# Two-block transformer in one kernel: the idle TensorE products between the stages are removed

## The chip, the cores and the metric

The kernel runs on one core of one Trainium2 chip. The metric is device microseconds of one execution, as a median over runs; smaller is better.

## The reference

Two blocks work on x of 256 tokens by 1024 channels, all in fp32. Cut to what matters here:

```python
def first_block(x, c, ...):
    for layer in range(2):
        shift, scale, gate = split(c @ mod_w[layer, 0] + mod_b[layer, 0], 3)
        h = rms_norm(x, norm_w[layer, 0, 0]) * (1.0 + scale) + shift
        y = mixer_ab(h, ...) if layer % 2 == 0 else mixer_cd(h, ...)
        x = x + gate * rms_norm(y, norm_w[layer, 0, 1])
        shift, scale, gate = split(c @ mod_w[layer, 1] + mod_b[layer, 1], 3)
        h = rms_norm(x, norm_w[layer, 1, 0]) * (1.0 + scale) + shift
        x = x + gate * rms_norm(swiglu(h, ffn_w_in[layer], ffn_w_out[layer]), norm_w[layer, 1, 1])

def second_block(x, cond, ...):          # mod: nine vectors from silu(cond) @ w_mod + b_mod
    x = x + 0.5 * g1 * swiglu_2(modulate(rms_norm_2(x, ffn1_norm), sh1, sc1), ...)
    proj = modulate(rms_norm_2(x, mix_norm), sh2, sc2) @ w_in
    y_mix = concat(rms_norm_2(short_conv(proj)), rms_norm_2(s5_mixer(proj)))
    x = x + g2 * (y_mix @ w_out)
    x = x + 0.5 * g3 * swiglu_2(modulate(rms_norm_2(x, ffn2_norm), sh3, sc3), ...)
    return rms_norm_2(x, final_norm)
```

What counts here is the shape: seven stages (ab, f0, cd, f1, f2, in2, f3), and between each and the next a normalisation over the 1024 channels of every token, on which the whole next stage depends.

## The kernel before

**Weights.** All weights and the matrices of the conditioning vectors come as one stream of 1 MB pieces through five buffers (`raw`), issued by SyncE in the order of a plan. ScalarE copies a half of a piece into `HI` in a rounded fp32 format, VectorE subtracts it from the original into `LO`; six such pairs are held. The conditioning vectors (`MV`) are made on VectorE by products of a raw piece with the condition and a sum (L1417). A product of weight and activation is three products on TensorE: both parts of the weight with the high part of the activation, and the high part of the weight with its low part.

**Activations.** `X` holds the rows of tokens. `HB` holds the modulated activation as high half (`HH`) and low half (`HLo`), in eight slices of 128 channels by 256 tokens; `HDH` and `HDL` hold the two parts of the hidden activation of a feed-forward stage.

**A stage change.** `add_normed` (or `add_gated`) adds the stage's result to `X` on VectorE. Then `modulate` runs on all engines. TensorE waits for the last gated bank (`gy`), transposes the 16 blocks of `X` into PSUM as each half of the rows is ready, and then spreads the inverse root of each half (`dg`, made by VectorE as a diagonal in `RS`) over all partitions with a product by a constant matrix (`nones`); these two are called the spreads here. ScalarE copies each spread back (`RS`), VectorE scales slice k by it (`TMP`, L1496), ScalarE writes `HH[k]`, VectorE writes `HLo[k]` (L1491), and TensorE begins the next stage as the slices appear. A feed-forward stage (f0 to f3) begins with one weight pair taken slice by slice, six products a slice; cd and in2 begin with one half, three products a slice.

**Idle products.** Before, `modulate` of TensorE also ran products whose result nobody reads, in four places: ahead of the wait for the first half, ahead of the second half's transposes, ahead of the second spread, and behind it. Their numbers are `fill`: (6, 4, 5, 4) at f0, cd, f1 and f2, (2, 2, 4, 4) at in2 and f3; the last is left out at f0. Each is 128 by 128 times 128 by 512, into a bank of the four that all stages share in turn (`take`, `give`). They wait for nothing themselves.

**Order.** Every engine's program is written out by hand in one order; TensorE takes its products strictly in that order.

Of the kernel before, what the change touches and what calls it, by code (L numbers as in the profile page):

```python
# [190 lines left out]
def build(nc, xT, small, vecs, ssm, consts, firsts, WS, scratch, gates_out, out):  # L191
# [15 lines left out]
    with ctx:  # L207
        def sb(name, shape, dt=fp32):
            return ctx.enter_context(nc.sbuf_tensor(name, shape, dt))

        def tally(name):
            return Tally(nc, ctx, name)
# [11 lines left out]
        HH, HLo = HB[:, 0], HB[:, 1]  # L224
        nones = sb("nones", [128, 128])
        zeros = sb("zeros", [128, 128])
        zb = zeros[:, :].bitcast(mybir.dt.bfloat16)
# [7 lines left out]
        HDH = sb("HDH", [128, 3, 256], f32r)  # L235
# [7 lines left out]
        P, A, D, G = tally("pe_done"), tally("act_done"), tally("dve_done"), tally("pool_done")  # L243
# [7 lines left out]
        banks = Banks(NWORK)  # L251
# [7 lines left out]
        def C(n):  # L259
            o, w = co[n]  # L260
            return CN[:, o:o + w]
# [13 lines left out]
        def turned(k):  # L275

            return PS[:, k % 4, k // 4 * 256:k // 4 * 256 + 256]
# [20 lines left out]
        def flat(a):  # L298
            return a.rearrange("p a b -> p (a b)")
# [106 lines left out]
        def pe(e):  # L406
            w = Waits(e)
            walk = Walk(plan, units, where, order)
            idle = [0]
            opened = set()  # L410

            def mm(o, l, r, start, stop):
                return e.matmul(o, l, r, start=start, stop=stop, skip_group_check=True)  # L413

            def freed(key):
                return D.at(("free", key)) if ("free", key) in D.value else A.at(("free", key))

            def take(key):
                i = banks.take(key)
                last = banks.before[key]  # L420
                if last is not None and last[0] != "idle":
                    w.wait_ge(*freed(last))
                return PS[:, WORK0 + i, :]

            def busy_wide(n, src=HH):
                idle[0] += 1
                key = ("idle", idle[0])
                ps = take(key)
                for i in range(n):
                    mm(ps[:, :], src[:, 0, 0:128], flat(src[:, 0:2, :]), True, True)  # L430
                banks.give(key)

            def busy(n):
                idle[0] += 1
                key = ("idle", idle[0])
                ps = take(key)
                w.wait_ge(*G.at("zeros"))
                for i in range(2 * n):
                    mm(ps[:, 0:256], zb[:, 0:128], zb, True, True)
                banks.give(key)  # L440

            def mods(col):
                walk.mods(col)

# [87 lines left out]
                if last:  # L532
                    x.then_inc(*P.up(("sum", tag)))

            def modulate(tag, sc, fill=(0, 0, 0, 0)):

                mods(sc + 8)
                if tag != "ab":
                    busy_wide(fill[0])
                    w.wait_ge(*D.at(("gy", tag, 3)))  # L540
                for qt in range(2):
                    if tag == "ab":
                        w.wait_ge(*XIN.at("in"))
                        w.wait_ge(*CONST.at("in"))
                    elif qt:
                        busy_wide(fill[1])
                    for k in range(8):
                        if tag != "ab" and k % 4 == 0:
                            w.wait_ge(*D.at(("x", tag, qt, k // 4)))
                        e.transpose(turned(k)[:, qt * 128:qt * 128 + 128], X[:, qt, k * 128:k * 128 + 128], C("ident"))  # L550
                for qt in range(2):
                    if qt and tag != "ab":
                        busy_wide(fill[2])
                    ps = take(("rb", tag, qt))
                    w.wait_ge(*D.at(("dg", tag, qt)))
                    mm(ps[:, 0:128], nones[:, :], dg[:, qt, :], True, True).then_inc(*P.up(("rb", tag, qt)))
                    banks.give(("rb", tag, qt))
                if tag not in ("ab", "f0"):
                    busy_wide(fill[3], HDH)

            def ffn(tag, slow, gcol):
                def down(j):
# [99 lines left out]
            def out_half(name, ks, qt, gives=1, begins=0):  # L662

                def half_ready(k):
                    wt = weight((name, k // 2), k % 2)
                    w.wait_ge(*A.at(("hh", name, k)))
                    w.wait_ge(*D.at(("hlo", name, 7 if qt or begins else max(k, 3))))
                    if begins and not qt:
                        w.wait_ge(*D.at(("hlo", name, 3)))
                    return wt  # L670

                ends = ks[-1] == 7 and qt == gives
                for k in ks[:-2] if ends else ks:
                    wt = half_ready(k)
                    rows(name, (HH, HLo), k, wt, k == begins, k == 7, [used((name, k // 2), k % 2)] if qt == gives else [],
                         (qt,))
                if ends:
                    wts = [half_ready(k) for k in ks[-2:]]
                    for h in range(2):
                        for k, wt in zip(ks[-2:], wts):  # L680
                            rows(name, (HH, HLo), k, wt, k == begins, k == 7,
                                 [used((name, k // 2), k % 2)] if h else [], (qt,), (h,))
# [4 lines left out]
            for q, oh in enumerate(("ohA", "ohB")):  # L687
                ps = take(("tab", q))
# [3 lines left out]
            walk.catch_up(walk.at_unit[4, 1])  # L692
            w.wait_ge(*G.at("consts"))
            modulate("ab", 8)

            for n in range(6):
# [3 lines left out]
            ps = take("gates")  # L700
            w.wait_ge(*D.at("gatew"))
            for k in range(8):
                mm(ps[0:24, 0:256], wgh[:, k, :], HH[:, k, :], k == 0, False)
                mm(ps[0:24, 0:256], wgl[:, k, :], HH[:, k, :], False, False)
                i = mm(ps[0:24, 0:256], wgh[:, k, :], HLo[:, k, :], False, k == 7)
            i.then_inc(*P.up("gates"))
            banks.give("gates")
            ps = take("gates2")
            w.wait_ge(*A.at(("free", "gates")))
            w.wait_ge(*CONST.at("in"))  # L710
            for qt in range(2):
                i = e.transpose(ps[:, qt * 24:qt * 24 + 24], ge[:, qt * 128:qt * 128 + 128], C("ident")[0:24, 0:24])
# [88 lines left out]
            out_half("abo", (0, 1), 1)  # L801
            out_half("abo", (6, 7), 0)
            out_half("abo", range(2, 8), 1)
            modulate("f0", 32, (6, 4, 5, 4))
            ffn("f0", lambda j: None, 40)

            opened.clear()
            modulate("cd", 56, (6, 4, 5, 4))
            for i in range(6):
                linear_fm(("cd", i), H2, "cd", 8, 2)  # L810

# [61 lines left out]
            out_half("cdo", (4, 5), 0, 0, 4)  # L873
            out_half("cdo", (0, 1, 2, 3, 6, 7), 0, 1, 4)
            out_half("cdo", (0, 1, 2, 3, 6, 7), 1, 1, 4)
            modulate("f1", 80, (6, 4, 5, 4))

            def turn(j):
                if j in (5, 6, 9, 10, 13, 14, 17, 18):
# [19 lines left out]
                    banks.give("kk")  # L899

            ffn("f1", turn, 88)
            modulate("f2", 104, (6, 4, 5, 4))
            ffn("f2", lags, 112)
            modulate("in2", 128, (2, 2, 4, 4))

            def drive():

# [50 lines left out]
            ps = take(("xs", "conv"))  # L958
# [8 lines left out]
            ps = take(("xs", "ssmy"))  # L967
# [2 lines left out]
            banks.give(("xs", "ssmy"))  # L970
            out_half("o2", range(4, 8), 0)
            out_half("o2", range(4, 8), 1)
            modulate("f3", 152, (2, 2, 4, 4))
            ffn("f3", lambda j: None, 160)

        def act(e):
# [1200 lines left out]
        for engine in (pe, act, dve, pool, sp):  # L2177
            engine(Counting())
# [5 lines left out]
        @block.tensor  # L2184
        def _(e):
            pe(e)
# [162 lines left out]
```

## Time and profile before

| | |
|---|---|
| median of 3 runs | 1234.2 us (1233.76 to 1235.08) |
| profiled execution | span 1233.6 us; the page gives no time of its own beside it |
| TensorE busy | 1145.4 us, 93% |
| VectorE busy | 957.4 us, 78% |
| ScalarE busy | 602.1 us, 49% |
| mean granted clock of TensorE | 0.976 |

The busy share of TensorE is by modelled ends of pipelined products; the start-to-start distance of rows tells more. The granted clock is given as a share of full speed: 1.00 is 2.4 GHz, 0.50 is 1.2 GHz, and a share between them is a stretch in which it changed. In the timeline a row may merge several instructions (x6); its second number is from the first start to the last end.

### The profile page before, as it was taken

What the parts mean: (1) busy time and instruction counts of PE and PEld (TensorE: products, weight loads), DVE (VectorE), ACT (ScalarE), POOL (GpSimd) and SP (SyncE); (2) the same over time, 40 slices, a digit from 0 to 9 for tenths busy, and PEclk for the clock granted to TensorE, in tenths of its full rate; (3) what the DMA queues carried; (4) which work ended last, traced back from release to release, by engine and by line L of the source; (5) the groups of instructions that cost most, each with busy time, mean ns of one, the idle gap of its engine ahead of it and who ended that gap; (6) DMA issues with size and microseconds to landing.
All of it is one profiled execution on the core that took longest, in us unless ns stands there. A gap on an engine that the chain in (4) does not pass through costs nothing.

```text
span 1233.6 us, 19573 instructions
## 1 busy us (share of the span) xinstructions
PE 1145.4 (93%) x8036; PEld 1023.9 (83%) x8036; DVE 957.4 (78%) x1710; ACT 602.1 (49%) x1055; POOL 69.4 (6%) x106
## 2 busy tenths in 40 slices
PE   2697899899999998999999999999999989999996
PEld 1696578899897996898998989999979968888885
DVE  5888868898887966788888778887776867777655
ACT  2434755444356457644344564344453365555543
POOL 1000000000000000185000000000000000000000
PEclk8799899999999999999999999999999999999998
DMA  9993334778882960367889637888723552666731
GB/s 374 358 391 126 133 127 181 305 304 312 290 336 108 368 263 21 131 261 273 306 245 360 249 108 277 327 283 313 302 94 126 111 181 86 217 260 253 183 128 35
DMA packets 41097, 280.74 MB, mean 228 GB/s; under 512 B 4768, under 2 KB 5296, under 8 KB 8240
## 3 DMA queue, kind: packets, MB, share of 16 engines
q1 hardware_dynamic: 37584, 269.27, 59.7%
q0 software_dynamic: 2416, 7.92, 2.0%
q10 hardware_dynamic: 1008, 2.30, 0.6%
q8 instruction: 63, 1.03, 0.3%
q14 instruction: 26, 0.21, 0.1%
HBM read 277.85 MB, written 1.10 MB: 226 GB/s over the span
## 4 chain that ended last, share of the span: by engine, by line
PE 64%; DVE 23%; ACT 6%; DMA 5%; issue 2%; SPq 0%; DVEq 0%; ACTq 0%
PE PS L413 64%; DVE LO L1427 7%; DMA raw<-WS 5%; DVE raw L1417 5%; ACT HI L981 3%; DVE TMP L1496 1%; DVE HB L1491 1%; DVE SC L1659 1%; ACT SQ L981 1%; DVE FB L1615 1%; DVE TMP L1533 1%; DVE TMP L1775 1%; DVE X L1538 1%; DVE SC L1644 1%; ACT HB L981 1%
## 5 line engine op out<-in xcount | busy, mean ns | idle before, releaser
L413 PE MATMUL PS<-HB,HI 128*128 128x256 f32 (+1 forms) x3160 | 648.2, 298 | 28.7 <-ACT HB L981 18.6
L413 PEld LDWEIGHTS PS<-HB,HI 128*128 128x128 f32 x3160 | 509.6, 192 | 57.0 <-ACT HB L981 21.1
L413 PE MATMUL PS<-HB,LO 128*128 128x256 f32 x1748 | 494.2, 283 | 0.0
L1427 DVE TENSOR_TENSOR LO<-raw,HI 128x1024 fp32r<-128x1024 f32 x340 | 404.1, 1226 | 92.7 <-ACT HI L981 92.6
L981 ACT ACTIVATE HI<-raw 128x1024 fp32r<-128x1024 f32 x340 | 338.5, 1047 | 91.6 <-DMA raw<-WS 44.9
L413 PEld LDWEIGHTS PS<-HB,LO 128*128 128x128 f32 x1748 | 334.8, 192 | 2.7
L1417 DVE CUSTOM_DVE_ANT_0 raw<-raw,CB,SM 128x1024 f32<-128x1024 f32 x168 | 209.9, 1284 | 18.9 <-DMA raw<-WS 18.8
L981 ACT ACTIVATE HDH<-FB 128x256 fp32r<-128x256 f32 x88 | 36.8, 418 | 243.9 <-DVE FB L1615 220.3
L413 PE MATMUL PS<-HI,HDH 128*128 128x512 f32 x352 | 140.2, 398 | 0.0
L413 PE MATMUL PS<-HI,HDL 128*128 128x512 f32 x352 | 139.4, 396 | 0.0
L413 PE MATMUL PS<-LO,HDH 128*128 128x512 f32 x352 | 139.1, 395 | 0.0
L413 PE MATMUL PS<-HI,HB 128*128 128x512 f32 (+2 forms) x352 | 91.6, 349 | 7.0 <-DVE HB L1516 5.9
L413 PEld LDWEIGHTS PS<-HI,HDL 128*128 128x128 f32 x352 | 66.4, 189 | 16.0
L1618 DVE TENSOR_TENSOR HDL<-FB,HDH 128x256 fp32r<-128x256 f32 x88 | 37.9, 430 | 51.6 <-ACT HDH L981 51.6
L413 PEld LDWEIGHTS PS<-HI,HDH 128*128 128x128 f32 x352 | 66.4, 189 | 13.5
L413 PEld LDWEIGHTS PS<-LO,HDH 128*128 128x128 f32 x352 | 66.4, 189 | 12.9
L413 PEld LDWEIGHTS PS<-HI,HB 128*128 128x128 f32 x352 | 62.2, 194 | 17.5 <-ACT HB L981 6.4
L981 ACT ACTIVATE FB<-PS 128x256 f32<-128x256 f32 (+1 forms) x115 | 45.2, 393 | 46.5 <-PE PS L413 46.2
L981 ACT ACTIVATE SC<-PS 128x512 f32<-128x512 f32 (+3 forms) x57 | 31.4, 567 | 63.5 <-PE PS L413 52.1
L413 PE MATMUL PS<-LO,HB 128*128 128x512 f32 (+2 forms) x176 | 61.0, 347 | 0.0
L2068 POOL DMA_DIRECT2D gates_out<-GV x7 | 6.4, 921 | 602.6 <-DVE GV L1511 343.4
L413 PE MATMUL PS<-SC 128*64 128x256 f32 (+4 forms) x336 | 36.3, 363 | 2.6 <-DVE SC L1659 1.5
(233 smaller groups left out, 925.0 us busy)
## 6 DMA issues: line engine op xcount, KB each, us to landing
raw<-WS SPq DMA_DIRECT2D x255, 1024.0 KB, 5.4
SC<-scratch POOLq DMA_DIRECT2D x2, 1024.0 KB, 16.0
FB<-gates_out POOLq DMA_DIRECT2D x3, 512.0 KB, 5.0
SQ<-gates_out POOLq DMA_DIRECT2D x3, 512.0 KB, 9.2
X<-xT ACTq DMA_DIRECT2D x1, 1024.0 KB, 6.8
SC<-ssm POOLq DMA_DIRECT2D x2, 512.0 KB, 3.8
out<-TMP SPq DMA_DIRECT2D x4, 256.0 KB, 2.6
CB<-vecs SPq DMA_DIRECT2D x1, 512.0 KB, 6.5
```

What stands on the lines that cost most here:

```text
L413: return e.matmul(o, l, r, start=start, stop=stop, skip_group_check=True)
L981: return e.activation(o, a, f, **k)
L1417: e.tensor_tensor_reduce(x, x, CB[:, :], 1.0, S("mb")[:, c:c + 1], O.mult, O.add, MV[:, c:c + 1]) \
L1427: e.tensor_tensor(LO[:, s % HL, :], raw_half(j, h), HI[:, s % HL, :].bitcast(fp32), O.subtract).then_inc(*D.up(("lo", s)))
L1491: e.scalar_tensor_tensor(HLo[:, k, :], TMP[:, k, :], MV[:, sh + k:sh + k + 1], HH[:, k, :].bitcast(fp32), O.add, O.subtract).then_inc(*D.u ...
L1496: e.scalar_tensor_tensor(TMP[:, k, :], turned(k), AV[:, k:k + 1], RS[:, 3, :], O.mult, O.mult) \
L1533: e.tensor_tensor(gy[b // 2][:, c], PS[:, b, :], grow(tag)[:, c], O.mult).then_inc(*D.up(("gy", tag, b)))
L1538: e.scalar_tensor_tensor(X[:, qt, c], gy[qt][:, c], r_n[:, qt:qt + 1], X[:, qt, c], O.mult, O.add) \
L1615: e.tensor_tensor(HF[:, j % 2, :], SIL[:, j % 2, :], bank((key, 0))[:, 256:512], O.mult) \
L1618: e.tensor_tensor(HDL[:, j % 3, :], HF[:, j % 2, :], HDH[:, j % 3, :].bitcast(fp32), O.subtract) \
L1644: e.tensor_scalar(s3[:, n, :], s3[:, n, :], gg[:, n:n + 1], None, O.mult) \
L1659: e.tensor_tensor_reduce(s3[:, n, :], bank(("s", tag, i))[:, n * kw:(n + 1) * kw], reverse(BI[:, bh + h0 + n, 0:kw]), 1.0, sk[:, n:n + 1] ...
```

## The change

`modulate` on TensorE no longer takes `fill`, and runs no idle product. Both helpers, `busy_wide` and the unused `busy`, are deleted. Nothing else is edited.

```diff
-            def busy_wide(n, src=HH):
-                idle[0] += 1
-                key = ("idle", idle[0])
-                ps = take(key)
-                for i in range(n):
-                    mm(ps[:, :], src[:, 0, 0:128], flat(src[:, 0:2, :]), True, True)
-                banks.give(key)
...
-            def modulate(tag, sc, fill=(0, 0, 0, 0)):
+            def modulate(tag, sc):
 
                 mods(sc + 8)
                 if tag != "ab":
-                    busy_wide(fill[0])
                     w.wait_ge(*D.at(("gy", tag, 3)))
                 for qt in range(2):
                     if tag == "ab":
                         w.wait_ge(*XIN.at("in"))
                         w.wait_ge(*CONST.at("in"))
-                    elif qt:
-                        busy_wide(fill[1])
                     for k in range(8):
...
                 for qt in range(2):
-                    if qt and tag != "ab":
-                        busy_wide(fill[2])
                     ps = take(("rb", tag, qt))
...
-                if tag not in ("ab", "f0"):
-                    busy_wide(fill[3], HDH)
...
-            modulate("f0", 32, (6, 4, 5, 4))
+            modulate("f0", 32)
...
-            modulate("in2", 128, (2, 2, 4, 4))
+            modulate("in2", 128)
```

The order of TensorE at the change to f2, before: the last products of f1 (those that read HDH with HI or LO), then idle products (reading HB or HDH alone) among the transposes (CN,X) and the spreads (RS,nones), then the first products of f2.

```order
L413 MATMUL PS<-HI,HDL 128x512
L413 MATMUL PS<-HB 128x512 x6
L550 MATMUL PS<-CN,X 128x128 x8
L413 MATMUL PS<-HB 128x512 x4
L550 MATMUL PS<-CN,X 128x128 x8
L413 MATMUL PS<-RS,nones 128x128
L413 MATMUL PS<-HB 128x512 x5
L413 MATMUL PS<-RS,nones 128x128
L413 MATMUL PS<-HDH 128x512 x4
L413 MATMUL PS<-HB,HI 128x256
```

The same place of the change:

```order
L413 MATMUL PS<-HI,HDL 128x512
L530 MATMUL PS<-CN,X 128x128 x16
L413 MATMUL PS<-RS,nones 128x128 x2
L413 MATMUL PS<-HB,HI 128x256
L413 MATMUL PS<-HB,LO 128x256
```

Nineteen products are gone there, and nothing has moved in their place. The change to f3, before, on TensorE, between the last product of the mixer's output and the first of f3:

```order
L413 MATMUL PS<-HI,HB 128x512
L413 MATMUL PS<-HB 128x512 x2
L550 MATMUL PS<-CN,X 128x128 x8
L413 MATMUL PS<-HB 128x512 x2
L550 MATMUL PS<-CN,X 128x128 x8
L413 MATMUL PS<-RS,nones 128x128
L413 MATMUL PS<-HB 128x512 x4
L413 MATMUL PS<-RS,nones 128x128
L413 MATMUL PS<-HDH 128x512 x4
```

And of the change:

```order
L413 MATMUL PS<-HI,HB 128x512
L530 MATMUL PS<-CN,X 128x128 x16
L413 MATMUL PS<-RS,nones 128x128 x2
L413 MATMUL PS<-HB,HI 128x256
L413 MATMUL PS<-HB,LO 128x256
```

Twelve products are gone there. The other engines' instructions and waits are the same, in the same order.

## Rows read from the trace of the kernel before

**Rows 1.** The page: its head, and the chain's shares by engine.

```profile
span 1233.6 us, 19573 instructions
...
PE 64%; DVE 23%; ACT 6%; DMA 5%; issue 2%; SPq 0%; DVEq 0%; ACTq 0%
```

**Rows 2.** The chain in order of time: start us, us, what (longest pieces).

```profile
200.00 1.20 DVE raw L1417
...
317.31 13.53 DMA raw<-WS
...
522.80 3.58 DVE LO L1427 x3
...
718.25 190.70 PE PS L413 x1383
...
1049.33 174.07 PE PS L413 x904
```

**Rows 3.** Instructions by tile, HB and HDH, TensorE: duration ns min/median/max.

```profile
L413 PE MATMUL PS<-HB x76: 387/393/481, 183.6 to 1034.6; 128*128 128x512 f32 x76
...
L413 PE MATMUL PS<-HDH x20: 387/397/478, 393.1 to 1035.8; 128*128 128x512 f32 x20
```

**Rows 4.** Stretches: length, busy PE, PEld, DVE, ACT, POOL, clock, DMA, GB/s.

```profile
44.80:48.10 3.30, 2.12 (x11) 1.34 (x11) 3.12 (x7) 3.02 (x6) 0.00 (x0) 1.00 0.84 348
48.20:51.50 3.30, 3.30 (x17) 3.30 (x17) 3.30 (x5) 1.85 (x2) 0.00 (x0) 0.50 0.72 253
...
709.90:718.20 8.30, 7.32 (x40) 5.32 (x38) 5.66 (x21) 4.80 (x18) 0.00 (x0) 1.00 0.00 0
```

**Rows 5.** Timeline at the change to f2: second spread, its reader, first product.

```profile
716.16 0.49 PE L413 MATMUL PS<-RS,nones 128*128 128x128 f32 x2
...
716.69 0.28 ACT L981 ACTIVATE RS<-PS 128x128 f32<-128x128 f32 x1 [1.23 <-PE PS L413]
...
718.25 0.36 PE L413 MATMUL PS<-HB,HI 128*128 128x256 f32 x1 [0.68 <-ACT HB L981]
```

**Rows 6.** Timeline at the start, low clock: second spread and its reader.

```profile
26.21 0.80 PE L413 MATMUL PS<-RS,nones 128*128 128x128 f32 x2 [1.13 <-DVE RS L1477]
27.04 0.28 ACT L981 ACTIVATE RS<-PS 128x128 f32<-128x128 f32 x1 [1.55 <-PE PS L413]
```

**Rows 7.** Timeline of TensorE in stage ab at the low clock.

```profile
41.78 0.41 PE L413 MATMUL PS<-HB,LO 128*128 128x256 f32 x1
...
42.57 0.42 PE L413 MATMUL PS<-HB,LO 128*128 128x256 f32 x1
...
48.43 0.63 PE L413 MATMUL PS<-HB,HI 128*128 128x256 f32 x2
...
49.07 0.63 PE L413 MATMUL PS<-HB,HI 128*128 128x256 f32 x2
```

**Rows 8.** Timeline of TensorE in f2: first pair by slices, then unheld.

```profile
720.29 0.47 PE L413 MATMUL PS<-HB,HI 128*128 128x256 f32 x2
...
721.07 0.47 PE L413 MATMUL PS<-HB,HI 128*128 128x256 f32 x2
...
724.58 0.40 PE L413 MATMUL PS<-HB,HI 128*128 128x256 f32 x2
...
724.94 0.40 PE L413 MATMUL PS<-HB,HI 128*128 128x256 f32 x2
```

**Rows 9.** Timeline at the change to in2: second spread's input and its product.

```profile
912.52 0.28 DVE L1477 TENSOR_SCALAR RS<-CN,NR 128x128 f32<-128x128 f32 x1
...
913.16 0.38 PE L413 MATMUL PS<-RS,nones 128*128 128x128 f32 x2
```

**Rows 10.** Timeline: f0's first reader, and waits of TensorE in f1, f3.

```profile
201.97 0.36 ACT L981 ACTIVATE FB<-PS 128x256 f32<-128x256 f32 x1
...
572.19 0.36 PE L413 MATMUL PS<-HB,HI 128*128 128x256 f32 x1 [1.66 <-DVE LO L1427]
...
1049.33 0.50 PE L413 MATMUL PS<-HB,HI 128*128 128x512 f32 x1 [0.24 <-DVE FB L1615]
```

More of the change, by code:

```diff
@@ L423, in take @@
                 return PS[:, WORK0 + i, :]
-            def busy_wide(n, src=HH):
-                idle[0] += 1
-                key = ("idle", idle[0])
-                ps = take(key)
-                for i in range(n):
-                    mm(ps[:, :], src[:, 0, 0:128], flat(src[:, 0:2, :]), True, True)
-                banks.give(key)
[L433 to L440, printed above, removed]
             def mods(col):
@@ L803, in pe @@
             out_half("abo", range(2, 8), 1)
-            modulate("f0", 32, (6, 4, 5, 4))
+            modulate("f0", 32)
             ffn("f0", lambda j: None, 40)
             opened.clear()
-            modulate("cd", 56, (6, 4, 5, 4))
+            modulate("cd", 56)
             for i in range(6):
@@ L875, in pe @@
             out_half("cdo", (0, 1, 2, 3, 6, 7), 1, 1, 4)
-            modulate("f1", 80, (6, 4, 5, 4))
+            modulate("f1", 80)
             def turn(j):
@@ L901, in pe @@
             ffn("f1", turn, 88)
-            modulate("f2", 104, (6, 4, 5, 4))
+            modulate("f2", 104)
             ffn("f2", lags, 112)
-            modulate("in2", 128, (2, 2, 4, 4))
+            modulate("in2", 128)
             def drive():
@@ L972, in pe @@
             out_half("o2", range(4, 8), 1)
-            modulate("f3", 152, (2, 2, 4, 4))
+            modulate("f3", 152)
             ffn("f3", lambda j: None, 160)
```

## The prediction

> **What bounds the kernel now.** I read the page first, for the bound; then the chain in order of time, for which engine carries it in each stage; then, at the six stage changes, the timeline of each engine and the granted clock by stretches. The page puts 64% of the chain on TensorE and 23% on VectorE [rows 1]. The chain in order tells the stages apart [rows 2]. In stage f2 TensorE carries it for 190.70 us without a break, and in f3 for the last 174.07 us: a microsecond lost there is lost for good. In f0 and f1 it runs over VectorE right behind the stage change (VectorE's conditioning products at 200.00, low halves of weights at 522.80), and in f0 later over a weight transfer of 13.53 us. There TensorE has time to spare.
>
> At a stage change TensorE has nothing of use to do for 8.30 us (f2, 709.90 to 718.20) but 16 transposes and two spreads, and the idle products fill the rest; the clock stays at 1.00 throughout [rows 4]. There are 96 idle products, 76 that read HB and 20 that read HDH [rows 3].
>
> **The change, part by part.** No engine but TensorE has another instruction or another wait. What is left of the gap is 16 transposes and two spreads of two passes each.
>
> *Does the clock fall?* The nearest rows are at the program's start [rows 4]. From 44.80 to 48.10 TensorE ran 11 products of 256 columns, busy for 2.12 us by the profile and idle for 1.18 us in all, and from 48.20 to 51.50 its clock was 0.50. Eleven products of 0.11 us of streaming (256 columns at 2.4 GHz) are 1.2 us of work in 3.3 us. At f2 the gap will hold 16 transposes and 4 passes of 128 columns, 20 x 0.053 = 1.1 us of work in 8.30 us: less than half of that density. So I take it that the clock falls at all six changes; at in2 and f3, whose gaps are some 2 us shorter, it falls late. The Trainium skill ("TensorE: Matmul & The Clock Gate", section "Why this matters for your kernels") warns only of idle gaps longer than any that this change leaves; by it alone the clock would stay up. The start rows speak against that, since 1.18 us without work, among thin work, was enough there.
>
> *Term A, the spread.* The second spread stands on the chain at every change: ScalarE waits for it, VectorE for ScalarE. At the full clock it takes 716.16 to 716.69, 0.53 us [rows 5]; at the low clock, at the start, 26.21 to 27.04, 0.83 us [rows 6]. That is 0.30 us more. At f2 it comes 6.3 us into the gap (709.90 to 716.16), and much the same at f0, cd and f1; I take the clock to be low by then. In cd and f2 it is lost in full. In f0 and f1 the chain meets later stalls that may swallow it (the 13.53 us transfer); I take half. Together 0.30 x 2 + 0.15 x 2 = 0.90 us. Bounds: 0 (clock still up) and 1.8 (six times).
>
> *Term B, the first weight pair of f2.* Six products belong to each of the eight slices of the modulated activation, and VectorE releases the slices: the same product stands at 720.29 and 721.07, 0.78 us a slice. Unheld, three products take 0.36 us (724.58 to 724.94), so 0.72 us a slice [rows 8]. At the low clock three products take 0.64 us (48.43 to 49.07) [rows 7], so 1.28 us a slice. With the clock low for D us after the first product, the pair ends at D + (8 - D/1.28) x 0.72 = 5.76 + 0.44 D; released by VectorE it ends at 7 x 0.78 + 0.72 = 6.18. The loss is 0.44 D - 0.42. The low stretch from 48.20 took 3.3 us, and the one before it reached from ahead of 41.78 to 44.80 at most; I bound D by 4.0. At f2 part of the low stretch will be over when work begins, so I take 3.0: 0.90 us. Bounds: 0 (D up to 1) and 1.34 (D of 4.0).
>
> *Term C, the same pair of f3.* Same sum, 0.90 us, less a stall that it fills: behind the third weight pair TensorE now idles 0.24 us until VectorE frees a bank [rows 10]. So 0.66 us. Bounds 0 and 1.1.
>
> *The same pairs of f0 and f1* cost nothing. In f0 the first reader of the result, ScalarE's at 201.97, stands behind other work of ScalarE and does not wait for TensorE; in f1 TensorE itself idles 1.66 us for a low half of weights at 572.19 [rows 10]. If that cover were gone, each would cost as much as f2's, 0.9 us.
>
> *cd and in2* begin with three products a slice, 0.64 us at the low clock, under the 0.78 us of the release. The start shows it: at the low clock the same product stands at 41.78 and 42.57, 0.79 us apart [rows 7]. Cost 0.
>
> *Term D, what the idle products hold up.* In in2 VectorE has the second spread's input at 912.52 + 0.28 = 912.80, but TensorE begins it at 913.16, behind idle products [rows 9]; without them it would follow at once, for which I allow 0.05 us. So 0.31 us is won, and the same at f3, where the timeline reads alike: -0.62 us together. At f2 nothing is held. Bounds: -0.62, and 0 if the clock is already low there.
>
> **Sum.** 0.90 + 0.90 + 0.66 - 0.62 = +1.84 us. On the profiled execution, of which the page gives only the span, that is 1233.6 to 1235.4 us; the median of the runs, 0.6 above the span, goes from 1234.2 to 1236.0 us, 0.15% more. Ends: all bounds low -0.6 (1233.6), all high 1.8 + 1.34 + 1.1 = +4.2 (1238.4).
>
> The Trainium skill weighs it otherwise: the same page, section "Terms", prices low clock at the throttled time times one minus the ratio, so half of it. With 3.3 us for each of six stretches that is six times 1.65, about 9.9 us, against the 1.84 of the rows. The start rows disagree for cd and in2: 0.79 us a slice at the low clock where f2 has 0.78 at the full one.
>
> **The rivals.**
>
> *All of it passes (slower).* The low stretch of every change delays the end by half its length, as if nothing were released or waited for elsewhere: 6 x 3.3 / 2 = 9.9 us, 1244.1 us. For it: in f2 and f3 the chain is all TensorE. Against: VectorE carries the chain in f0 and f1, and releases the slices in cd and in2. It decides where a slice at the low clock outlasts the release by much and no wait follows.
>
> *Cover is thinner than it looks (slower).* The pairs of f0 and f1 pass on to the end (2 x 0.9), and the spread's 0.30 passes in full (2 x 0.15): 1.84 + 2.1 = +3.9, 1238.1 us. For it: in f1 TensorE is nearly full as well, ahead of that wait. Against: up to 572 the timelines of f1 name no wait of ScalarE or VectorE on TensorE. It decides from a delay beyond 1.66 us in f1.
>
> *The clock stays up (no change by measure).* Transposes and spreads are enough to keep it. Then only term D is left: 1233.6 us. For it: the gap is broken up by that work, with no long pause left in it. Against: the fall at 48.2.
>
> *Idle products disturb others (faster).* If they slow VectorE's or ScalarE's steps in the gap, these get shorter. VectorE is busy for 5.66 us of f2's gap [rows 4]; a tenth of that, six times, is 3.4 us: 1230.8 us. No row shows such a slowing.
>
> **How the numbers follow.** Repeated runs lie within about 0.1% (1233.76 to 1235.08), and about 0.2%, 2.5 us, is what a measurement of this kernel can tell from no change. The sum as worked out: 0.50. Clock stays up: 0.13. Thinner cover: 0.23. All passes: 0.10. Faster: 0.04. Within 0.2% falls the forecast but for a tail of 0.04, and the clock that stays up, 0.59 in all; slower 0.23 + 0.10 + 0.04 = 0.37; faster 0.04. The range goes from 1233.4 (clock up) to 1238.8 (thinner cover), and leaves out the first and the last rival and some edge. The likeliest case alone: 1234.8 to 1237.2. Predicted: 1236.0 us.
>
> **What would show it.** In the profile of the changed kernel: no product that reads HB or HDH alone; a clock of 0.50 in stretches that begin inside the six gaps and end a few microseconds after the first weight product; 0.83 us from the second spread to ScalarE at f0, cd, f1, f2 (A); first pairs of f2 and f3 of about 7 us instead of 6.2 (B, C); in cd and in2 slices of 0.79 us at either clock; in in2 and f3 the second spread 0.05 us behind VectorE (D); in f0 and f1 the waits for low halves shorter by as much as the first pair got longer. Wrong it would be by a clock of 1.00 in the gaps, by low stretches of 6 us and more after work begins, by a second fall while slices are still being released, or by a wait in f0 or f1 of ScalarE or VectorE on TensorE that is not there now.

## The result and the profile after

| | before | changed |
|---|---|---|
| first comparison, median of 5 runs each | 1234.2 us (1233.55 to 1235.08) | 1239.33 us (1237.98 to 1240.87) |
| ratio, with its 95% interval | | 1.0032 [1.0019, 1.0046] |
| the same kernel again, 12 runs | 1235.71 us (35 runs) | 1238.54 us, ratio 1.0020 [1.0005, 1.0035] |
| a third time, 11 runs | 1236.08 us (23 runs) | 1237.6 us, ratio 1.0012 [1.0003, 1.0021] |

The forecast was 1236.0 us, with a range up to 1238.8. The first comparison lies above it. The three ratios, weighted by the inverse square of their intervals, give 1.0019 [1.0012, 1.0025]: some 2.3 us of 1234.2, against the 1.84 of the sum. The second and the third were taken on different chips, and the intervals of the first and the third overlap by little, so the pooled one is rough. Both halves of that need explaining: why the first comparison showed 5.1 us between the medians, and whether 2.3 us came about as the prediction had it.

The profiled execution of the changed kernel took 1239.33 us, of which 1237.5 lie in the span, so 1.8 us lie around it. Before, I had only a span of 1233.6 [rows 1] and a median 0.6 above it; if 1.8 us lie around that span too, that execution took 1235.4 us, and the two profiles differ by 3.9 us only. The page of the changed kernel, its head and the chain's shares:

```profile
span 1237.5 us, 19376 instructions
...
PE 61%; DVE 25%; DMA 6%; ACT 6%; issue 2%; SPq 0%; DVEq 0%; ACTq 0%
```

TensorE's share of the chain is 61% where it was 64%. The chain in order of time, for the pieces that answer to [rows 2]: start, length, what.

```profile
318.46 14.07 DMA raw<-WS
...
720.08 192.69 PE PS L413 x1383
...
1053.30 174.07 PE PS L413 x904
```

The same 1383 products of f2 take 192.69 us instead of 190.70: 1.99 us, half of the whole difference, in one row. The 904 products of f3 take 174.07 in both, and they start 3.97 us later. The weight transfer at 318 took 14.07 us instead of 13.53; nothing in the change touches it.

The stretches at the change to f2, which answer to [rows 4]: length, busy time of PE, PEld, DVE, ACT and POOL, granted clock, DMA.

```profile
711.90:720.00 8.10, 3.43 (x21) 2.29 (x20) 5.51 (x20) 4.60 (x18) 0.00 (x0) 0.94 0.00 0
719.10:722.40 3.30, 2.32 (x10) 2.30 (x11) 3.11 (x8) 1.93 (x4) 0.00 (x0) 0.50 0.00 0
722.50:725.80 3.30, 3.30 (x17) 3.30 (x17) 3.12 (x9) 2.42 (x5) 0.00 (x0) 0.50 0.00 0
725.90:729.20 3.30, 3.30 (x29) 3.30 (x29) 1.69 (x3) 3.27 (x4) 0.00 (x0) 1.00 0.18 22
```

TensorE is busy for 3.43 us of the gap, where the idle products had made it 7.32. The clock falls at the very end of the gap, about 719.0, and is still 0.50 in the second low row, although TensorE had work all through it (3.30 of 3.30). It is back at 725.9. The first product of f2 starts at 720.08, so the clock is low for 5.8 us of work. The timeline there, of TensorE and of ScalarE's reader, beside [rows 5] and [rows 8]:

```profile
718.08 0.49 PE L413 MATMUL PS<-RS,nones 128*128 128x128 f32 x2 [1.02 <-DVE RS L1453]
718.61 0.28 ACT L957 ACTIVATE RS<-PS 128x128 f32<-128x128 f32 x1 [1.23 <-PE PS L413]
720.08 0.58 PE L413 MATMUL PS<-HB,HI 128*128 128x256 f32 x1 [1.51 <-ACT HB L957]
...
721.41 0.63 PE L413 MATMUL PS<-HB,HI 128*128 128x256 f32 x2
...
722.69 0.63 PE L413 MATMUL PS<-HB,HI 128*128 128x256 f32 x2
...
726.24 0.40 PE L413 MATMUL PS<-HB,HI 128*128 128x256 f32 x2
...
726.60 0.40 PE L413 MATMUL PS<-HB,HI 128*128 128x256 f32 x2
```

The spread still ran at the full clock here (0.53 us to ScalarE, as before). Then a slice takes 1.28 us (721.41 to 722.69), which is the price that the prediction read from the start of the program, and three products are back at 0.36 us from 726.24. At cd the spread came late enough to meet the low clock (VectorE's input, the spread, the reader):

```profile
394.18 0.29 DVE L1453 TENSOR_SCALAR RS<-CN,NR 128x128 f32<-128x128 f32 x1
394.52 0.80 PE L413 MATMUL PS<-RS,nones 128*128 128x128 f32 x2 [0.68 <-DVE RS L1453]
395.35 0.28 ACT L957 ACTIVATE RS<-PS 128x128 f32<-128x128 f32 x1 [1.20 <-PE PS L413]
```

That is 0.83 us, to the hundredth what [rows 6] gave. At in2 the spread now follows its input by 0.05 us (916.33 + 0.29 = 916.62, then 916.67), where [rows 9] had 0.36. The last row below is the stall of f3 that answers to [rows 10]: 0.23 us where it was 0.24.

```profile
916.33 0.29 DVE L1453 TENSOR_SCALAR RS<-CN,NR 128x128 f32<-128x128 f32 x1
916.67 0.49 PE L413 MATMUL PS<-RS,nones 128*128 128x128 f32 x2 [0.94 <-DVE RS L1453]
...
1053.30 0.49 PE L413 MATMUL PS<-HB,HI 128*128 128x512 f32 x1 [0.23 <-DVE FB L1591]
```

The stretches at cd, f1, in2, and the gap and first pair of f3:

```profile
391.40:401.50 10.10, 7.86 (x30) 6.89 (x31) 7.89 (x23) 5.85 (x15) 0.00 (x0) 0.50 0.00 0
510.90:521.00 10.10, 7.92 (x33) 7.31 (x34) 7.89 (x24) 5.84 (x15) 0.53 (x1) 0.50 0.15 52
920.50:923.70 3.20, 3.14 (x13) 2.73 (x12) 3.20 (x9) 2.09 (x5) 0.00 (x0) 0.50 0.00 0
1034.20:1040.70 6.50, 2.99 (x22) 2.30 (x20) 4.46 (x16) 3.51 (x12) 0.53 (x1) 1.00 0.21 81
1040.80:1046.80 6.00, 5.98 (x45) 5.71 (x46) 5.59 (x14) 4.07 (x8) 0.00 (x0) 1.00 0.02 4
```

At cd and f1 the clock is low for 10.1 us in a row, three times the 3.3 that the prediction went by. At f3 it does not fall at all, in a gap with 2.99 us of busy TensorE in 6.50.

### The profile page after: what moved, and what is told of

Same layout as the page of the kernel before. It is cut to its first block, busy times and chain, and to the rows that moved or that the text cites. A ratio compares the mean times of both kernels' runs of the same rounds, so it can differ in the third digit from the quotient of the medians.

```text
span 1237.5 us, 19376 instructions
## 1 busy us (share of the span) xinstructions
PE 1137.1 (92%) x7940; PEld 1020.1 (82%) x7940; DVE 956.7 (77%) x1710; ACT 603.7 (49%) x1055; POOL 69.5 (6%) x106
## 4 chain that ended last, share of the span: by engine, by line
PE 61%; DVE 25%; DMA 6%; ACT 6%; issue 2%; SPq 0%; DVEq 0%; ACTq 0%
PE PS L413 60%; DVE LO L1403 8%; DVE raw L1393 6%; DMA raw<-WS 6%; ACT HI L957 3%; DVE TMP L1472 1%; DVE SC L1635 1%; DVE HB L1467 1%; PE PS L612 1%; ACT SQ L957 1%; DVE FB L1591 1%; DVE TMP L1509 1%; DVE X L1514 1%; ACT HB L957 1%; ACT HDH L957 1%
## 5 line engine op out<-in xcount | busy, mean ns | idle before, releaser
L413 PEld LDWEIGHTS PS<-HB,HI 128*128 128x128 f32 x3160 | 515.4, 194 | 55.0 <-ACT HB L957 24.9
L413 PEld LDWEIGHTS PS<-HB,LO 128*128 128x128 f32 x1748 | 338.9, 194 | 2.7
L413 PE MATMUL PS<-SC 128*64 128x256 f32 (+4 forms) x336 | 38.8, 380 | 3.1 <-DVE SC L1635 1.5
## 6 DMA issues: line engine op xcount, KB each, us to landing
SQ<-gates_out POOLq DMA_DIRECT2D x3, 512.0 KB, 10.2
```

## The experiments

Each was compared with the kernel before on the same chip (e1 to e4 on one, a2 and e5 to e7 on a second, a3, e8 and b2 on a third); the diffs are against the kernel before. One table serves them all. It splits every profiled execution into stages, at the start of the last weight product of each stage, so that a gap belongs to the stage behind it (f3 ends with the last product of the program; o2 is in2 and the mixer's output). A star marks a stage whose idle products were left out or cut.

```
kernel    ab ends     f0      cd      f1      f2      o2      f3
before     183.41  202.90  118.75  204.57  198.92  121.41  193.03
e1         182.76  203.01  118.45  204.37  198.90  121.36  193.04
b2         184.39  203.06  118.35  204.59  198.93  121.20  192.85
e2         183.68  203.01  118.39  204.58  200.85* 121.47  193.04
e3         182.06  203.32* 118.20  205.05* 198.89  122.34  193.03
e4         184.72  204.13  118.34* 204.47  198.89  121.17* 193.42*
e5         182.21  203.03  118.53  204.90  199.69* 122.22  193.05
e6         183.81  203.06* 119.00* 205.43* 198.91  120.76* 193.38*
e7         183.36  203.54  118.42  204.51  198.92  119.36* 193.58*
e8         182.31  203.00  118.71  204.60  200.83* 121.93  193.04
changed    184.63  203.37* 118.93* 204.63* 200.80* 121.76* 192.84*
a2         185.82  203.29* 118.83* 205.16* 200.66* 121.27* 192.85*
a3         184.04  203.34* 118.26* 204.89* 200.63* 121.34* 192.76*
```

f2 is the clearest column: 198.89 to 198.93 us in the seven profiles with all its idle products, 200.63 to 200.85 in the five that lack those around the second spread (with or without the earlier ones), and 199.69 in e5, which lacks the earlier ones alone. Stage ab, ahead of every edit, ends anywhere from 182.06 to 185.82. The columns f0, cd, f1 and o2 scatter too where nothing of them was edited: f0 from 202.90 to 204.13, cd from 118.20 to 118.75, f1 from 204.37 to 204.90, o2 from 121.20 to 122.34.

**e1, the kernel before once more.** A copy, no edit.

> The kernel before once more, for a second profile. Theory: 1.2 us of the change's 5.1 us are no effect of the change but where the clock falls in stage ab, which no idle product precedes; then this profile has low stretches in stage ab at other places than the first profile of it, and f0's first product comes at a time that differs from the first profile's by 0.5 to 1.5 us. Rival: stage ab falls alike in every execution of this kernel and the changed kernel shifts it; then f0's first product stands within 0.2 us of the first profile's.

The first product of f0 came at 191.79 us, against 192.45 in the first profile of the kernel before. Stage ab ended 0.65 us earlier, and its long low stretches stood elsewhere (101.6 to 111.9 us and 118.7 to 125.5, against 123.3 to 130.1). So where the clock falls in stage ab differs between executions of one kernel; that much of the theory holds. The execution took 1234.3 us, with a span of 1232.5.

**e2, left out at f2 alone.**

```diff
-            modulate("f2", 104, (6, 4, 5, 4))
+            modulate("f2", 104)
```

> The idle products left out at the change to f2 alone. Theory (terms A and B with the low stretch lasting 5.8 us behind the first product, as the trace of the change has it): 0.30 + 0.44 x 5.8 - 0.42 = +2.4 us, 1.0020 of the kernel before, with a clock of 0.50 for 6 to 7 us from about 1 us after f2's first weight product or around it. As predicted (low for 3.0 us behind it): +1.2 us, 1.0010. Rival, all of a low stretch passes: half of 6.8 us, +3.4 us, 1.0028. Rival, the clock stays up: 0.

Ratio 1.0013 [1.0004, 1.0022], 1.6 us. The clock was low from the gap until 723.7 us, 5.1 us past the first product of f2 (718.58). The stretch of that work, and the chain's piece that it opens:

```profile
718.60:723.60 5.00, 5.00 (x23) 5.00 (x24) 5.00 (x13) 3.06 (x7) 0.00 (x0) 0.50 0.02 3
```

```profile
718.58 192.35 PE PS L413 x1383
```

The ratio alone does not choose between the theory's 1.0020 and the prediction's 1.0010; the rows do: 192.35 - 190.70 = 1.65 us for the pair and 0.30 us more gap make the 1.95 of the table. The formula of term B gives 0.44 x 5.1 - 0.42 = 1.82. The clock that stays up is excluded; that all of the low stretch passes (3.4 us) lies outside the interval.

**e3, left out at f0 and f1 alone.**

```diff
-            modulate("f0", 32, (6, 4, 5, 4))
+            modulate("f0", 32)
...
-            modulate("f1", 80, (6, 4, 5, 4))
+            modulate("f1", 80)
```

> The idle products left out at the changes to f0 and f1 alone. Theory: the first weight pairs are covered, by ScalarE's other work in f0 and by the wait for a low half of weights in f1, and only half of the second spread's 0.30 us is left at each: +0.3 us, 1.0002, with the wait in f1 at the low half of weights shorter by the lag of the first pair. Rival, the cover is thinner: 2 x (0.30 + 0.90) = +2.4 us with the low stretch as predicted, up to 2 x 2.4 = +4.8 us with that of f2, 1.002 to 1.004.

Ratio 1.0002 [0.9994, 1.0011]. Here both second spreads met the low clock (both gaps were 0.30 us longer), and both first pairs ran at it, for 4 to 5 us. The wait in f1 shows where the rest went:

```profile
571.00 0.36 PE L413 MATMUL PS<-HB,HI 128*128 128x256 f32 x1 [0.75 <-DVE LO L1427]
```

It had been 1.66 us [rows 10], and is 0.75 here (0.57 in the changed kernel): TensorE came late, and waited less. From the first product of f1 to its last the stage took 195.62 us, against 195.24 to 195.46 in the three profiles of the kernel before. The cover held but for 0.2 to 0.4 us. The rival's +2.4 us and more lies outside the interval (up to +1.4).

**e4, left out at cd, in2 and f3 alone.**

```diff
-            modulate("cd", 56, (6, 4, 5, 4))
+            modulate("cd", 56)
...
-            modulate("in2", 128, (2, 2, 4, 4))
+            modulate("in2", 128)
...
-            modulate("f3", 152, (2, 2, 4, 4))
+            modulate("f3", 152)
```

> The idle products left out at the changes to cd, in2 and f3 alone. Theory: 0.30 us for the second spread at cd, nothing for cd's and in2's first halves, -0.31 us each at in2 and f3 for the second spread that is no longer held up, and at f3 0 or 0.66 us as the clock falls there or not: -0.3 to +0.3 us, 0.9997 to 1.0003. Rival, all of the low stretches passes: cd 5.1 us, in2 1.7 us, f3 1.7 us, in all +5 to +8.5 us, 1.004 to 1.007. Rival, stage o2 and f3 pass on what in2 and cd lose: +1.5 us, 1.0012.

Ratio 0.9999 [0.9990, 1.0008]: the theory's 0.9997 to 1.0003, and neither rival. The gaps of in2 and f3 were 0.19 us shorter each (term D). And at f3 the clock did fall this time, but only behind the first product (1038.40):

```profile
1031.90:1038.30 6.40, 2.89 (x21) 2.29 (x20) 4.36 (x16) 3.51 (x12) 0.53 (x1) 1.00 0.24 82
1038.50:1039.60 1.10, 1.10 (x8) 0.94 (x8) 1.10 (x4) 0.55 (x2) 0.00 (x0) 1.00 0.03 7
1039.80:1043.00 3.20, 3.20 (x17) 3.20 (x17) 3.20 (x9) 2.04 (x4) 0.00 (x0) 0.50 0.00 0
```

In the middle row TensorE is at work without a pause at clock 1.00, and then it drops for the 3.2 us of the last row. From the first product of f3 to the last took 186.74 us, against 186.16: 0.58 us. That is term C, where the clock falls.

**a2, the changed kernel once more.** A copy, no edit.

> The changed kernel once more, with more rounds. Theory: of the first comparison's 5.1 us only the part that the stages behind a removed group show is the change's (f2 1.9, f0, cd, f1 and in2 0.2 to 0.4 each, f3 -0.2 to +0.4), the rest is where the clock falls in stage ab, which differs from one execution to the next of the kernel before too (its end at 182.1 to 184.7 us in five profiles): +2 to +3 us, 1.0016 to 1.0025. Rival, the whole 5.1 us is the change's: 1.0035 to 1.0045 again, and stage ab ends at 184.5 us or later again.

Ratio 1.0020 [1.0005, 1.0035], as the theory had it; but stage ab ended late again (185.82 us), as the rival had it, so the cause stayed open and a3 below repeats it. Its f2, and that of a3, as pieces of the chain:

```profile
721.93 192.25 PE PS L413 x1383
```

```profile
719.36 192.22 PE PS L413 x1383
```

1.55 and 1.52 us more than before, with a clock low for 4.8 us (until 726.7) and 4.7 us (until 724.1) behind the first product.

**e5, at f2 only the late idle products.**

```diff
-            modulate("f2", 104, (6, 4, 5, 4))
+            modulate("f2", 104, (0, 0, 5, 4))
```

> At the change to f2 the idle products ahead of the transposes left out (6 and 4), those around the second spread kept (5 and 4). Theory, only the clock behind f2's first weight product counts (term B): the 9 late products either keep it up, then 0, 1.0000, or they come too late to bring it back, then the 1.9 us of all being left out, 1.0016, with a clock of 0.50 over some 5 us behind the first product. Rival, what costs is the thin work of the whole gap: about half of it, +1 us, 1.0008.

Ratio 1.0006 [0.9991, 1.0021], too wide to choose; the trace chooses. f2 took 199.69 us, 0.79 more than before, and none of it behind the first product: the 1383 products took 190.71 us. The clock fell inside the gap and was back before them:

```profile
712.30:715.60 3.30, 3.30 (x14) 2.94 (x14) 2.10 (x9) 1.98 (x7) 0.00 (x0) 0.50 0.00 0
715.80:718.00 2.20, 1.60 (x8) 0.98 (x7) 0.93 (x3) 0.87 (x3) 0.00 (x0) 1.00 0.00 0
718.10:724.00 5.90, 5.90 (x44) 5.64 (x45) 5.55 (x14) 3.96 (x8) 0.00 (x0) 1.00 0.01 3
```

The rival's size, about 1 us, was near; what cost the 0.8 us neither had: the five idle products ahead of the second spread ran at the low clock, took 2.10 us and held the spread up. Its input was there at 714.86 + 0.29 = 715.15; it began at 716.08.

```profile
714.86 0.29 DVE L1477 TENSOR_SCALAR RS<-CN,NR 128x128 f32<-128x128 f32 x1
```

```profile
714.14 2.10 PE L413 MATMUL PS<-HB 128*128 128x512 f32 x5
716.08 0.38 PE L413 MATMUL PS<-RS,nones 128*128 128x128 f32 x2
```

**e6, left out everywhere but at f2** (the edits of e3 and e4 together).

> The change with the idle products of f2 kept, all others left out. Theory: f2 is the only change where they are worth anything; what is left is the second spread at f0, f1 and cd and the gain of term D: 0 to +0.9 us, 1.0000 to 1.0007. Rival, the parts pass on more together than alone (stage f0 and f1 lose their cover when cd and in2 come late): +2 us or more, 1.0016.

Ratio 1.0005 [0.9990, 1.0019], median 1235.81 against 1235.71: what the theory had, 0 to 0.9 us, but with +2 us (1.0016) inside the interval. The stages that carry a star sum, against the mean of the three profiles of the kernel before, to 203.06 + 119.00 + 205.43 + 120.76 + 193.38 - (202.99 + 118.52 + 204.51 + 121.32 + 192.97) = +1.3 us, of which f1 is 0.9.

**e7, more idle products where the clock falls in the kernel before, fewer where they hold up.**

```diff
-            modulate("in2", 128, (2, 2, 4, 4))
+            modulate("in2", 128, (2, 2, 2, 4))
...
+            busy_wide(6, HDH)
             linear_out("o2", range(4))
...
+            busy_wide(14, HDH)
             out_half("o2", range(4, 8), 0)
...
-            modulate("f3", 152, (2, 2, 4, 4))
+            modulate("f3", 152, (2, 2, 2, 4))
```

> The kernel before with more idle products, where its own trace has the clock fall: 6 ahead of the first and 14 ahead of the last four channel slices of the mixer's output (TensorE waits 1.94 us at 1000.13 and 3.91 us at 1017.63 there, and the clock is 0.50 for 3.4 us from each), and 2 in place of 4 ahead of the second spread of in2 and f3. Theory: both low stretches are on the chain of TensorE and cost half their length, 2 x 1.7 us, and term D gives 2 x 0.3 us: -4.0 us, 0.9968. Rival, what TensorE gains there it waits for again: only term D, -0.6 us, 0.9995. Rival, the added products hold up the slices: 0 or slower.

Ratio 0.9995 [0.9980, 1.0009]: the theory's 4 us did not come; median 1234.63 against 1235.71. The two low stretches are gone (in the kernel before the clock was 0.50 from 1000.5 and from 1017.6, 3.4 us each):

```profile
998.00:1001.00 3.00, 2.44 (x12) 1.74 (x11) 2.09 (x5) 0.81 (x2) 0.00 (x0) 1.00 0.01 3
1013.00:1017.30 4.30, 3.65 (x16) 2.66 (x15) 2.29 (x6) 1.31 (x3) 0.00 (x0) 1.00 0.78 318
1017.40:1021.00 3.60, 3.60 (x16) 2.97 (x17) 2.15 (x6) 1.60 (x4) 0.00 (x0) 1.00 0.00 0
```

Stage o2 became 2.0 us shorter and f3 0.6 us longer, because its gap grew to 7.42 us from 6.87: TensorE was done sooner, and its transposes waited 1.35 us for VectorE where they had waited 0.63. From the last product of f2 to the first of f3 it took 126.78 us, against 128.07 to 128.28 in the three profiles of the kernel before: 1.3 to 1.5 us less, of which 0.2 are in2's shorter gap and 0.29 the second spread of f3. So neither the theory's 4.0 us nor the rival's 0.6: TensorE waits again for the greater part of what the clock gives it.

**a3, the changed kernel a third time.** A copy, no edit.

> The changed kernel a third time, beside runs on another chip perhaps. Theory (the sum of what the changed stages showed: f2 1.9, cd 0.3, f1 0.5, o2 -0.5, f3 0.1, f0 0): +2.2 us, 1.0018, and stage ab, in which nothing differs, ends between 182 and 186 us as it falls out (182.1 to 184.7 us in the eight profiles of kernels that keep idle products at f2 or elsewhere, 184.6 and 185.8 in the two of the changed kernel). Rival, stage ab is really later in the changed kernel: its end at 184.5 us or later a third time, and +4 us, 1.0032.

Ratio 1.0012 [1.0003, 1.0021], with the theory's 1.0018 inside and the rival's 1.0032 outside. Stage ab ended at 184.04 us. The three changed profiles end it at 184.04 to 185.82, the three of the kernel before at 182.76 to 184.39, and the other seven, with the same program up to there, at 182.06 to 184.72.

**e8, at f2 only the early idle products.**

```diff
-            modulate("f2", 104, (6, 4, 5, 4))
+            modulate("f2", 104, (6, 4, 0, 0))
```

> At the change to f2 the 10 idle products ahead of the transposes kept, the 9 around the second spread left out. Theory (what counts is how long the clock is 0.50 behind the first weight product): the work just ahead of f2's first product is as thin as without any, so the clock falls at or behind that product and stays low for some 3.4 us or more behind it: stage f2 at 199.5 to 200.7 us against 198.9 with all of them, +0.6 to +1.8 us, 1.0005 to 1.0015. Rival, the early products are enough: 198.9 us, 1.0000.

Ratio 1.0012 [1.0004, 1.0021], and f2 at 200.83 us: the ten early products bought nothing at all.

```profile
709.00:716.10 7.10, 5.28 (x31) 3.82 (x29) 4.64 (x19) 4.09 (x16) 0.00 (x0) 1.00 0.00 0
716.30:717.20 0.90, 0.00 (x0) 0.00 (x0) 0.71 (x3) 0.61 (x2) 0.00 (x0) 0.50 0.00 0
717.30:722.90 5.60, 5.60 (x26) 5.60 (x27) 5.41 (x14) 3.66 (x8) 0.00 (x0) 0.50 0.01 3
```

```profile
717.24 0.55 PE L413 MATMUL PS<-HB,HI 128*128 128x256 f32 x1 [1.60 <-ACT HB L981]
...
717.24 192.62 PE PS L413 x1383
```

TensorE was busy for 5.28 of the first 7.10 us. Behind the second spread it stood still for 1.60 us, the clock fell in that pause, and then it was low for 5.8 us of full work (until 723.0). Loss 1.92 us, a little more than the 0.6 to 1.8 expected; the formula gives 2.13. The nine products behind the early ones are what f2 needs, and by e5 they need the early ones ahead of them.

**b2, the kernel before a third time.** A copy, no edit.

> The kernel before a third time, for a profile. Theory: stage ab ends anywhere between 182 and 186 us; f2 takes 198.9 us and f3 193.0 us as in the other profiles with all idle products there, and stage f1 204.4 to 204.6 us.

Stage ab ended at 184.39 us, f2 took 198.93, f1 204.59, and f3 192.85, 0.2 under what was expected. The execution took 1235.79 us, 1.5 us more than e1's of the same kernel, and stage ab's 1.63 us account for it. This kernel has all its idle products, and yet its clock fell behind the first products of f0 (193.43) and of in2 (915.91):

```profile
195.40:198.60 3.20, 3.20 (x17) 3.20 (x17) 3.20 (x9) 2.08 (x5) 0.00 (x0) 0.50 0.00 0
919.10:922.30 3.20, 3.20 (x13) 2.85 (x13) 2.55 (x7) 2.64 (x5) 0.00 (x0) 0.50 0.00 0
```

So did that of e2 at f0 (from 194.6) and that of e3 at in2 (from 916.5), which keep the products there.

## Why the prediction was right or wrong

**The size.** The range was exceeded by the first comparison, and not by the two later ones taken by their ratios (1234.2 x 1.0020 and x 1.0012 are 1236.7 and 1235.7 us). Of the 5.1 us between the first medians, the trace showed 1.2 us lost before f0 began, where the program is the same, and 0.5 us in one weight transfer. By the means of three profiles each, the stages behind that differ by f0 +0.3, cd +0.2, f1 +0.4, f2 +1.8, o2 +0.1 and f3 -0.2: together 2.6 us, which fits the pooled 2.3. That the rest was where the clock happened to fall in stage ab is not shown: the changed kernel's three ends of ab are 1.3 us later in the mean than those of the kernel before, 1.6 us later than the mean of all ten profiles in the rows above them in the table, of which only e4's is later than 184.63. Spreads of 1.6 to 1.8 us don't settle whether that is chance. The whole times speak for chance: 2.6 us behind ab and 1.3 in it would be 3.9, and the pooled interval ends at 3.1.

**Does the clock fall?** "At all six changes" held at f0, cd, f1, f2 and in2, in all three profiles, in the gap or up to 2 us behind it. It failed at f3: the clock stayed up there in all three, and fell at f3 in e4 and e6, which lack the same products there. So the same gap can go both ways. Nor do the idle products decide it alone: at cd, f1 and f2 no profile that keeps all of them shows a fall, but at f0 two of eight do (e2, b2), and at in2 two of seven (e3, b2). Those falls came 1.9 to 3.1 us behind the first product, and those at in2 in the changed kernel's profiles 1.1 to 1.7 us behind it.

**Term A** (0.90 us predicted). The price was right, 0.83 against 0.53 us. But often the spread ran before the fall: by the gaps, the mean over three profiles is 0.10 at f0, 0.12 at cd, 0.21 at f1 and 0.11 at f2, in all 0.54 us.

**Term B** (0.90) is the step that was mis-sized. Its formula, 0.44 D - 0.42, held to within 0.21 us, always on the high side: with the D that the traces show (5.8, 4.8, 4.7, 5.1 and 5.8 us in the changed kernel, a2, a3, e2 and e8) it gives 2.13, 1.69, 1.65, 1.82 and 2.13, and 1.99, 1.55, 1.52, 1.65 and 1.92 were measured. What failed is D itself: I took 3.0 us, bounded by 4.0, from the low stretches at the start, which took 3.3 us, and reasoned that part of one would be over when work begins. The low stretches at f2 were 6.8 to 10.2 us long in these five profiles. The trace of the kernel before had longer ones as well: one of 6.8 us from 123.3 in stage ab, which I had not taken in, and the one that ended at 44.80, of which I had taken only the end, from 41.78 on; it had begun at 20.9, though with TensorE busy for 5.54 of its 23.80 us.

```profile
20.90:44.70 23.80, 5.54 (x19) 4.69 (x20) 19.81 (x45) 7.61 (x18) 0.00 (x0) 0.50 1.02 402
...
123.40:130.00 6.60, 5.68 (x33) 4.01 (x33) 5.86 (x31) 3.63 (x12) 0.00 (x0) 0.50 0.99 418
```

With these in sight nothing bounded D by 4.0. The mean over the changed kernel's three profiles is 1.69 us, 0.79 more than predicted and beyond the bound of 1.34.

**Term C** (0.66) was not there in the changed kernel (0.01 to 0.09 us between the first and the last product of f3), because the clock stayed up. Where it fell, in e4, it was 0.58. Why it stayed up in the changed kernel and fell in e4 and e6 is open.

**The pairs of f0 and f1, and cd and in2** (0 predicted): right as far as the traces can tell. e3 shows the cover, in the wait in f1 that shrank from 1.66 to 0.75 us. From its first to its last product f1 took 195.29 to 195.82 us in the changed kernel's three profiles, and 195.77 in e5, where nothing of it was edited.

**Term D** (-0.62): -0.55, the gaps of in2 and f3 being 0.27 to 0.29 us shorter each, with the 0.05 us that was allowed.

**The sum.** 0.54 + 1.69 + 0.06 - 0.55 = 1.74 us where 1.84 was predicted, so the sum came out well by luck: B was 0.79 too small, C 0.60 and A 0.36 too large. The stages behind ab differ by 2.6 us, and the terms leave 0.9 of that open, mostly in f0, f1 and o2, whose scatter without any edit is as large.

**The rivals.** All of it passes (+9.9) is excluded. Thinner cover (+3.9) is what the first comparison looked like, but e3 shows that it is not what happened. The clock stays up is wrong but for f3. Idle products disturb others: no sign of it. ScalarE's reader of the spread takes 0.28 us with them [rows 5] and without, and between f1's last product and f2's second spread VectorE's 23 instructions take 5.10 us with them and 5.09 without, ScalarE's 18 take 4.40 in both.

**The rule of the Trainium skill** ("TensorE: Matmul & The Clock Gate", section "Why this matters for your kernels"), by which gaps as short as these would leave the clock up, was read with the transposes as work: TensorE's longest pause in the gap is 1.6 us at cd and f2 and 2.2 us at f1 in the changed kernel's profiles. So read, it does not fit the falls at cd, f1 and f2. If only products are counted as work, TensorE goes without one for 4.6 to 5.3 us at f0, cd, f1 and f2, and these changes don't test it. e8 speaks against it on either reading: there no pause in the gap was longer than 1.6 us, nor any stretch without a product, and the clock fell. The same page's section "Terms" would have the lost time at half of the low stretch; in f2 1.99 us of 6.8 were lost, so 29%.

## What to carry to other kernels

Work of no use that keeps a clock up is worth what TensorE would lose on the chain right behind the gap. In this kernel 19 of 96 products, at one change of six, were worth 1.8 us, and the other 77 could not be told from nothing (e6, from 1.2 us faster to 2.3 slower without them). Price a low clock by the work that stands on the chain while it lasts, and before taking how long it lasts from one low stretch, look at every low stretch of the trace and at the work that ran in it: here they were from 3.4 to 23.8 us long, and the prediction went by the shortest. Where one kernel's runs scatter by 2 us, compare stage by stage, over several profiles, before giving a difference of 5 us to an edit.

## What was not expected of the hardware

The clock stayed low long after TensorE was at full work: 5.6 us busy without a pause at 0.50 in e8, and a low stretch of 10.1 us at cd and f1. In e8 it fell in a pause of 1.60 us, after TensorE had been busy for 5.28 of 7.10 us. It also fell in the middle of dense work, 1.3 us after the first product of f3 in e4. And executions of one kernel place the falls differently: stage ab ended between 182.76 and 184.39 us in three executions of the kernel before.
